# Three layers of a mixed transformer on one core: the last attention with stationary values and distant transposes, and the first squares added without waiting for the constants

## The reference

```python
def rms_norm(x, gain):
    xf = x.astype(jnp.float32)
    y = xf * lax.rsqrt(jnp.mean(xf * xf, axis=-1, keepdims=True) + RMS_EPS)
    return (y * gain.astype(jnp.float32)).astype(x.dtype)
...
    mod = jax.nn.silu(c) @ w_ada + b_ada
    shift, scale, gate = jnp.split(mod, 3, axis=-1)
    h = rms_norm_2(x, norm_g) * (1 + scale[:, None, :]) + shift[:, None, :]
    proj = h @ w_in
    q, kcr, vcr, ksl, vsl, kwn, vwn, z_a, g_br, u, z_s = jnp.split(proj, offs, axis=-1)
    gates = jax.nn.sigmoid(g_br).reshape(B, T, N_HEADS, N_BRANCH)
    attn = nsa_attention(q, kc, vc, k_slc, kv_heads(vsl), k_win, kv_heads(vwn), gates)
    # per head: g[0] * softmax(q kc) vc + g[1] * softmax(q_r k_slc) v_slc + g[2] * softmax(q_r k_win) v_win
    attn = attn * jax.nn.silu(z_a)
    y = gelu(s5_mixer(u, ...))
    y = y * jax.nn.sigmoid(y @ glu_w + glu_b)
    ssm = y * jax.nn.silu(z_s)
    mix = jnp.concatenate([attn, ssm], axis=-1) @ w_out
    return x + gate[:, None, :] * mix
```

## Time and profile before

| | |
|---|---|
| three runs, us | 1848.31, 1845.28, 1842.94; median 1845.28 |
| the profiled execution, us | 1844.67 |
| its span, us | 1842.5 |
| TensorE busy | 1760.9 us, 96% |
| VectorE busy | 1165.5 us, 63% |
| ScalarE busy | 667.8 us, 36% |
| GpSimd busy | 101.3 us, 5% |
| mean DMA | 134 GB/s |
| slab products (L474) in the chain that ended last | 70% |

### The profile page before, as it was taken

One profiled execution on the slowest core, in us unless ns is written; L12 is line 12 of the kernel. 1 busy time (PEld: TensorE's weight loads), 2 busy tenths in 40 slices (PEclk: granted clock), 3 DMA queues, 4 the chain that ended last, 5 costly groups with the idle time before them and its releaser, 6 DMA issues.

```text
span 1842.5 us, 24232 instructions
## 1 busy us (share of the span) xinstructions
PE 1760.9 (96%) x9361; PEld 1465.6 (80%) x9361; DVE 1165.5 (63%) x2373; ACT 667.8 (36%) x1081; POOL 101.3 (5%) x194
## 2 busy tenths in 40 slices
PE   3998999999999999999999999999999998999999
PEld 2776768888888888878888898888888987777787
DVE  6777766876467656564454548874676579445574
ACT  3423673423232333233232335322323332366432
POOL 0001100001000100100000000010001100000000
PEclk9999999999999999999999999999999999999999
DMA  9354324335333534642323224354336222300351
GB/s 367 115 181 162 115 69 145 138 114 186 120 115 136 172 114 155 212 164 92 137 91 138 75 97 146 135 171 164 140 129 201 96 91 92 127 34 24 138 195 46
DMA packets 45470, 245.98 MB, mean 134 GB/s; under 512 B 6256, under 2 KB 6480, under 8 KB 27440
## 3 DMA queue, kind: packets, MB, share of 16 engines
q1 hardware_dynamic: 24848, 155.36, 23.3%
q0 software_dynamic: 20512, 89.11, 14.4%
HBM read 229.23 MB, written 15.22 MB: 133 GB/s over the span
## 4 chain that ended last, share of the span: by engine, by line
PE 81%; DVE 11%; ACT 3%; issue 2%; DMA 2%; SPq 0%; DVEq 0%; ACTq 0%
PE ps L474 70%; DVE w_lo L1480 2%; PE ps L935 2%; DMA ada_raw<-in_ada 1%; PE ps L809 1%; PE ps L916 1%; PE ps L925 1%; ACT w_hi L1050 1%; PE ps L644 1%; DVE ada_raw L1504 1%; PE ps L667 1%; PE ps L653 1%; DVE ada_first L1865 1%; DVE pre L1597 1%; PE ps L957 1%
## 5 line engine op out<-in xcount | busy, mean ns | idle before, releaser
L1480 DVE TENSOR_TENSOR w_lo<-w_raw,w_hi 128x2048 fp32r<-128x2048 f32 x136 | 311.6, 2291 | 153.8 <-ACT w_hi L1050 153.5
L1050 ACT ACTIVATE w_hi<-w_raw 128x2048 fp32r<-128x2048 f32 x136 | 260.0, 1912 | 361.7 <-PE ps L474 339.0
L474 PE MATMUL ps<-h_hi,w_hi 128*128 128x512 f32 (+1 forms) x1008 | 379.1, 376 | 9.9 <-DVE w_lo L1480 6.5
L474 PE MATMUL ps<-h_lo,w_hi 128*128 128x512 f32 (+1 forms) x1008 | 374.8, 372 | 0.0
L474 PE MATMUL ps<-h_hi,w_lo 128*128 128x512 f32 (+1 forms) x1008 | 374.5, 372 | 0.0
L474 PEld LDWEIGHTS ps<-h_hi,w_hi 128*128 128x128 f32 x1008 | 191.8, 190 | 43.7 <-DVE w_lo L1480 7.0
L474 PEld LDWEIGHTS ps<-h_hi,w_lo 128*128 128x128 f32 x1008 | 191.7, 190 | 32.6
L474 PEld LDWEIGHTS ps<-h_lo,w_hi 128*128 128x128 f32 x1008 | 191.8, 190 | 31.3
L474 PE MATMUL ps<-hid_hi,w_hi 128*128 128x512 f32 (+1 forms) x576 | 211.3, 367 | 0.0
L474 PE MATMUL ps<-hid_hi,w_lo 128*128 128x512 f32 (+1 forms) x576 | 210.6, 366 | 0.0
L474 PE MATMUL ps<-hid_lo,w_hi 128*128 128x512 f32 (+1 forms) x576 | 210.5, 366 | 0.0
(11 more groups left out here) (395 smaller groups left out, 2400.5 us busy)
## 6 DMA issues: line engine op xcount, KB each, us to landing
w_raw<-in_slabs SPq DMA_DIRECT2D x136, 1024.0 KB, 4.8
ada_raw<-in_ada POOLq DMA_DIRECT2D x104, 512.0 KB, 5.1
s_tables<-s_tab POOLq DMA_DIRECT2D x4, 2692.0 KB, 9.2
s_t<-s_tables POOLq DMA_DIRECT2D x4, 2692.0 KB, 9.8
ada_first<-in_ada SPq DMA_DIRECT2D x16, 512.0 KB, 15.1
a_bias<-in_a_bias POOLq DMA_DIRECT2D x16, 256.0 KB, 3.3
xT<-in_xT SPq DMA_DIRECT2D x4, 512.0 KB, 6.3
s_toeplitz<-KTp POOLq DMA_DIRECT2D x32, 64.0 KB, 3.3
```

What stands on the lines that cost most here:

```text
L474: last = mm(o, l, r, start=start and n == 0, stop=stop and n == 2)
L1050: A(w_hi[s][:], w_raw[:, s, :], ACT.Copy).then_inc(sem("hi_done"), 1)
L1480: tt(w_lo[s][:], w_raw[:, s, :], w_hi[s][:].bitcast(F32), ALU.subtract).then_inc(sem("lo_done"), 1)
```

## The change

At the start VectorE adds squares as soon as they are there, and waits for the constants only before the first product with an ada tile; ScalarE's wait for `ones` and `eps` moves behind the squares and the silu.

In the last attention the weights are scaled by inverse sum and gate on VectorE before they are turned (as in the first loop), the values become the stationary side with 64 columns, and both groups of a head pair go to the two halves of a bank's partitions. All branches of a head pair add up in the same bank, the compressed one as the last (`compressed_out`, with scaled weights and a block-diagonal `vblk`). So the result stands turned in PSUM, `h_o`, its sums and its 16 transposes go, and gate, high and low part of three of the four head pairs move into the loop. The transposes stand six steps behind the scores instead of three, the values eight instead of four; there are 8 buffers for the exponentials. Slab units are cut into two bursts of 12. The steps of the turns of u and of the compressed branch are set anew. Output part 0 comes before the first block's outputs, and the rest is dealt out as 1, 2, 2, 1 and 1.

```diff
-        SIDE_A, SIDE_H = Side([0, 8, 14, 20, 26, 30, 34, 38], TT, 2), Side([1, 11, 22, 33, 44, 55], 2)
+        SIDE_A, SIDE_H = Side([0, 8, 14, 20, 26, 30, 34, 38], TT, 2), Side([1, 11, 22, 33, 44, 55], 2, 2)
...
+        U_STEPS = {step: (n // 3, n % 3) for n, step in enumerate((8, 16, 18, 20, 27, 29, 38, 40, 49, 51, 58, 60))}
+        CMP_STEPS = {step: (n // 2, n % 2) for n, step in enumerate((6, 14, 25, 31, 36, 42, 47, 53))}
+        CMP_SCALE = {step + 4: i for step, (i, part) in CMP_STEPS.items() if part == 0}
+        OUT_STEPS = {16 * i + 22: i for i in range(4)}
+        ATT_PARTS = (1,), (2, 3), (4, 5), (6,)
...
                 elif b == 1:
-                    gp.wait_ge(sem("h_added"), 4)
+                    gp.wait_ge(sem("c_out"), 4)
...
+            def compressed_out(i):
+
+                pe.wait_ge(sem("side_free"), C_COPIED[i])
+                for it in range(TT):
+                    last = mm(ps[5 + i % 2][:, it * P:(it + 1) * P], vblk[:, it % 2, :], c_pt[i % 2][:, it // 2, :],
+                              start=False, stop=True, skip_group_check=True)
+                last.then_inc(sem("c_out"), 1)
...
-                u = s - 3
+                u = s - 6
                 if 0 <= u < NUH:
...
-                u = s - 4
-                if 0 <= u < NUH:
-                    i, it, br, g = UNITS_H[u]
-                    pe.wait_ge(sem("hpt_ready"), u + 1)
-                    if u % 4 == 0 and u >= 8:
-                        pe.wait_ge(sem("ho_done"), u // 4 - 1)
-                    o, vc = ps[5 + u // 4 % 2][:, (u % 4) * HD:(u % 4 + 1) * HD], slice((br - 1) * P + g * HD, (br - 1) * P + (g + 1) * HD)
+                u = s - 8
+                if u >= 0 and s % 2 == 0:
+                    i, it, br, _ = UNITS_H[u]
+                    pe.wait_ge(sem("hpt_ready"), u + 2)
+                    if u % 16 == 0 and i >= 2:
+                        pe.wait_ge(sem("hxo_gated"), i - 1)
                     for j in range(it + 1):
-                        last = mm(o, h_pt[:, u % 3, j * P:(j + 1) * P], hv[:, j, vc], start=j == 0, stop=j == it)
+                        for g in range(H_GROUPS):
+                            vc = slice((br - 1) * P + g * HD, (br - 1) * P + (g + 1) * HD)
+                            last = mm(ps[5 + i % 2][HD * g:HD * g + HD, it * P:(it + 1) * P], hv[:, j, vc],
+                                      h_pt[:, (u + g) % 3, j * P:(j + 1) * P], start=it == 0 and br == 1 and j == 0, stop=False, skip_group_check=True)
                     last.then_inc(sem("ho_full"), 1)
+                if s in OUT_STEPS:
+                    compressed_out(OUT_STEPS[s])
...
             states(0)
-            pe.wait_ge(sem("h_added"), 4)
-            for i in range(4):
-                transposes([h_o[:, t, i * P:(i + 1) * P] for t in range(TT)], "hxo_full")
+            attention_part(0)
...
-            act.wait_ge(sem("ones_set"), 2)
             for k in range(KT):
...
             silu(0)
+            act.wait_ge(sem("ones_set"), 2)
+            A(stat[:, 8:9], eps[:], ACT.Sqrt)
             act.wait_ge(sem("consts_in"), 80)
-            A(stat[:, 8:9], eps[:], ACT.Sqrt)
...
-            dve.wait_ge(sem("consts_in"), 80)
-            dve.wait_ge(sem("ones_set"), 2)
             for k in range(1, KT):
...
             dve.wait_ge(sem("cond_done"), 1)
+            dve.wait_ge(sem("consts_in"), 80)
+            dve.wait_ge(sem("ones_set"), 2)
             first_pair(0)
...
+                u = s - 3
+                if 0 <= u < NUH and s % 2:
+                    i, it, br, _ = UNITS_H[u]
+                    n, h2 = P * (it + 1), slice(u % 8, u % 8 + 2)
+                    dve.wait_ge(sem("he_done"), u + 2)
+                    step(V.reciprocal(row_inv[:, h2], row_sum[:, h2]))
+                    step(tt(h_w[:, h2], row_inv[:, h2], h_gts[:, it, 6 * i:6 * i + 6].rearrange("p (g b) -> p g b", b=N_BR)[:, :, br], ALU.mult))
+                    for v in (u, u + 1):
+                        ts_(h_p[:, v % 8, 0:n], h_p[:, v % 8, 0:n], h_w[:, v % 8:v % 8 + 1], None, ALU.mult).then_inc(sem("hp_ready"), 1)
+                if s - 2 in OUT_STEPS:
+                    i = OUT_STEPS[s - 2]
+                    dve.wait_ge(sem("za_done"), 1)
+                    dve.wait_ge(sem("c_out"), i + 1)
+                    if i:
+                        dve.wait_ge(sem("hx_done"), i)
+                    tt(h_gate[:], ps[5 + i % 2][:], za[:, i, :], ALU.mult).then_inc(sem("hxo_gated"), 1)
+                if s - 4 in OUT_STEPS:
+                    i = OUT_STEPS[s - 4]
+                    dve.wait_ge(sem("hxo_hi"), i + 1)
+                    tt(o_lo[:, i, :], h_gate[:], o_hi[:, i, :].bitcast(F32), ALU.subtract).then_inc(sem("hx_done"), 1)
```

More of the change, by code:

```diff
@@ L349, in program @@
         ZA_READ = len(SIDE_A.starts) + 1 + H_USES.index(SIDE_H.starts[1]) + 1
+        C_COPIED = [len(SIDE_A.starts) + 1 + H_USES.index(step) + 1 for step, (i, part) in CMP_STEPS.items() if part == 1]
         SIDE_ALL = len(SIDE_A.starts) + 1 + len(H_USES)
@@ L902, in compressed @@
                     last.then_inc(sem("c_turned"), 1)
[L903 to L908, removed]
+            def compressed_out(i):
[4 more added lines that the diff above has]
+                last.then_inc(sem("c_out"), 1)
+            for s in range(NUH + 7):
                 if s < NUH and s % 2 == 0:
@@ L994, in _ @@
             states(0)
[L995 to L997 removed]
+            attention_part(0)
+            c.add("bank", 4)
             for blk in range(NBLK):
@@ L1387, in place_z @@
                 return za[:, 2 + u, :] if u < 2 else zs[:, u - 2, :]
-            for s in range(NUH + 3):
+            for s in range(NUH + 10):
                 side(SIDE_H, s, place_z)
@@ L2179, in _ @@
             kc = ps[7][0:CMP_PAD, :].rearrange("n (k g d) -> n k g d", k=4, d=HD)
-            step(cp(kcn[:], kc[:, 0, :, :]), *[cp(vblk[CMP_PAD * r:CMP_PAD * (r + 1), r, :], kc[:, 1, r % 2, :]) for r in range(4)])
+            step(cp(kcn[:], kc[:, 0, :, :]), *[cp(vblk[CMP_PAD * r:CMP_PAD * (r + 1), r // 2, HD * (r % 2):HD * (r % 2) + HD], kc[:, 1, r % 2, :]) for r in range(4)])
             V.engine_nop().then_inc(sem("side_free"), 1)
@@ L2184, in _ @@
             dve.wait_ge(sem("gts_done"), 1)
-            for s in range(NUH + 7):
+            for s in range(NUH + 11):
                 if s < NUH:
@@ L2207, in _ @@
                     V.engine_nop().then_inc(sem("side_free"), 1)
-                if s - 1 in CMP_STEPS:
-                    i, part = CMP_STEPS[s - 1]
+                if s - 1 in CMP_STEPS and CMP_STEPS[s - 1][1] == 0 or s in CMP_SCALE:
+                    i, part = (CMP_SCALE[s], 1) if s in CMP_SCALE else CMP_STEPS[s - 1]
                     cs = c_s[:].rearrange("p (j n) -> p j n", n=CMP_PAD)
@@ L2243, in _ @@
-                q = (s - 8) // 4
-                if s >= 8 and s % 4 == 0 and q < NUH // 4:
-                    i, it = UNITS_H[4 * q][0:2]
-                    dve.wait_ge(sem("hw_done"), q + 1)
-                    dve.wait_ge(sem("ho_full"), 4 * q + 4)
-                    step(tt(h_q4[:], ps[5 + q % 2][:, 0:256].rearrange("p (j d) -> p j d", d=HD),
-                            h_w[:, q % 2, :, :].rearrange("p b g -> p (b g)").unsqueeze(2).to_broadcast([P, 4, HD]), ALU.mult))
-                    tt(h_o[:, it, i * P:(i + 1) * P].rearrange("p (g d) -> p g d", d=HD), h_q4[:, 0:2, :], h_q4[:, 2:4, :], ALU.add)\
-                      .then_inc(sem("ho_done"), 1)
-                    dve.wait_ge(sem("ho_done"), q + 1)
@@ L2307, in _ @@
             recurrence(0)
-            dve.wait_ge(sem("za_done"), 1)
-            for i in range(5):
-                if i < 4:
-                    dve.wait_ge(sem("hxo_full"), i + 1)
-                    if i >= 2:
-                        dve.wait_ge(sem("hx_done"), i - 1)
-                    tt(h_gate[:, i % 2, :], ps_of(c)[:], za[:, i, :], ALU.mult).then_inc(sem("hxo_gated"), 1)
-                    c.add("bank")
-                if i:
-                    dve.wait_ge(sem("hxo_hi"), i)
-                    free(V.engine_nop())
-                    tt(o_lo[:, i - 1, :], h_gate[:, (i - 1) % 2, :], o_hi[:, i - 1, :].bitcast(F32), ALU.subtract).then_inc(sem("hx_done"), 1)
-            dve.wait_ge(sem("hx_done"), 4)
+            attention_part(0)
+            free(V.engine_nop(), 4)
+            c.add("bank", 4)
             for blk in range(NBLK):
```

109 lines of the change are left out of this document (39 added, 70 removed).

## The result

The changed kernel takes **1834.93 us** in the median of five runs (1833.21 to 1838.22), the kernel before 1845.28 (1842.94 to 1849.24): ratio 0.9937, 95% interval 0.9925 to 0.995. That is faster by about 10 us. The forecast was 1830.5, 1823 to 1838, so the time lies inside, 4.4 us above the point.

The account below looks back on a forecast made before the run. The prediction took TensorE, four fifths of the chain that ended last, as the bound. Start -4.1, last loop -8.5 and the stretch behind it -1.5 took 1844.67 to 1830.6, stated as 1830.5 us, range 1823 to 1838.

Parts of the forecast that it names:

- Start, -4.1: Start of the kernel: VectorE's adds no longer wait for the constants, and the shift reaches TensorE, -4.1 us.
- Rival 2: Start gives nothing, since a later transfer comes at its old time and VectorE waits for it: 1834.6 us, chance 0.06.
- Values, -13.4: Last attention loop: 320 value products of 128 columns in pairs replace 320 of 64 columns on TensorE, 35.8 to 22.4 us.
- Rival 4: Last loop: pairs overlap completely and changes between groups are free, 18.2 off instead of 7.9: 1820.3 us, chance 0.02.
- Transposes, +5.5: Last loop: 160 transposes in 64 groups get dearer on TensorE beside products in column halves, 21.4 to 26.9 us.
- Compressed and bursts, -1.4 and +0.6: Last loop: three compressed groups at 0.9 each stay, one leaves, -1.4 us; cutting six slab units adds six group changes, +0.6.
- Waits, +0.2: Last loop: TensorE's idle time, 6.1 us before, goes slightly up by 0.2, bounds -4 and +8.
- VectorE, 83 of 128: Last loop: VectorE has 83 us of work in some 128, covered by TensorE unless waited for step by step.
- Rival 3: Last loop: VectorE becomes the bound, waiting for ScalarE in each pair of steps; slower, for example 1852.3 us, chance 0.03.
- Rival 1: Middle of the last loop: VectorE's wait for exponentials sets the pace, waits of +8: 1838.4 us, chance 0.13.
- Rival 5: Last loop has the waits of the first attention loop or fewer, -3: 1827.6 us, chance 0.16.
- Behind the loop, -1.5: After the last loop: the second block's outputs start 23.15 us behind the last value instead of 24.7, -1.5 us.

Follow-up runs that it names:

- e1: The kernel before with only the start's edit (the moved waits for the constants and ones): 1842.44 us, ratio 0.9973.
- e12: The kernel of e2 run again, beside the changed kernel on the same chip: 1830.98 us, ratio to before 0.9914.
- e5: The changed kernel with the values' products of one group all before those of the other, not alternating between partition halves: 1841.9 us, ratio to before 0.9969.
- e7: The kernel of e2 with each slab unit as one burst of 24 products instead of two of 12: 1831.67 us, ratio to before 0.9925.
- e8: The kernel of e2 with each of VectorE's 64 weight scalings preceded by another of the same size by 1.0: 1839.3 us, ratio to before 0.9958.
- e2: The changed kernel with ScalarE's silu of z_a moved from step 14 to step 22 of the last loop: 1832.42 us, ratio to before 0.9917.
- e10: The kernel of e2 with transposes four steps behind the scores instead of six, values six instead of eight: 1835.33 us, ratio to before 0.9945.
- e3: The kernel before with the silu of z_a moved from step 13 to step 22 of the last loop: 1846.02 us, ratio 0.9986.
- e11: The changed kernel itself run again, nothing altered: 1835.8 us, ratio to before 0.9948.

## Why the prediction was right or wrong

**Start, -4.1, right.** Measured -3.6 at the first slab product and -3.9 at the loop, in most other profiles -4.0 to -4.1 at the product; e1 has it by itself. Rival 2, a transfer behind it, is out.

The terms of the loop can be measured one by one: TensorE's time from the first start of each group to that of the next, idle time taken out, added up by line from the first scores to the last value product. For the work I take e12, whose clock doesn't fall a second time; the last two rows are the changed kernel's own.

| term | forecast | before, us | after, us | change |
|---|---|---|---|---|
| values | -13.4 | 35.8 | 22.3 | -13.5 |
| transposes | +5.5 | 21.1 | 25.0 | +3.9 |
| compressed products | -1.4 | 4.05 | 2.9 | -1.2 |
| slab bursts | +0.6 | 35.3 | 36.4 | +1.0 |
| other work | 0 | 35.1 | 35.2 | +0.1 |
| waits | +0.2 | 7.0 | 9.9 | +2.9 |
| half clock at the silu | none | 0 | 2.6 | +2.6 |

**Values, -13.4, right.** 1.03 per sixteen. Rival 4, the pairs at 0.055 and changes between groups free, is out: a group of sixteen costs 1.03 and not 0.88. The Trainium skill, TensorEngine Tiling (Array Packing), section Theoretical Speedup, gives up to 2x for a side of 64 or less. The traces agree with the bound: in pairs a product takes 0.055 where one by itself takes 0.109 (e5), and a whole group of sixteen gains less, 1.03 for the 1.79 of before.

**Transposes, +5.5, too much by 1.6.** Four take 0.58 and no surplus appears in the pairs, but the 0.15 per group, read beside products in column halves, was taken for all 64 groups, and over the whole loop it is some 0.12.

**Compressed and bursts, -1.4 and +0.6, each off by 0.2 to 0.4** (1.00 for 0.9 a group; for the cut e7 has 0.3 in the loop).

**Waits, +0.2: this step failed.** It took the waits of before, 6.1, as a sum that moves little, and looked at the first loop for a sample. But 2.03 of them were one event, the silu of z_a with its table loads, which stands at a step and is covered by what TensorE has at that step. The change moved both: its text names the new steps of the turns of u and of the compressed branch, but not that of the silu, and neither text nor forecast asks what the silu would stand beside. The first loop has no such event, so it was no sample for it. Measured: waits of 4.06 instead of 2.03, and behind them 2.6 for the clock, 4.6 of added cost. The other waits rose by 0.9, where 0.2 was forecast; they moved from the readers of bank 7 (1.4, 0.5, 0.3 and 0.3 before) to VectorE's masks (2.9 after).

**The clock was not in the sum.** Each wait was priced at its length. At the silu 0.86 and 1.17 with 1.33 of work between them cost no more (before, and in e1 likewise); 1.89 and 2.17 with 0.52 of work between them cost 2.6 more.

**Some luck in the number.** Too dear transposes hid 0.9 of the miss, net of the other terms of work: waits and clock came 5.3 above the forecast, the loop 4.4.

**VectorE, 83 of 128, right:** 79.5. Rival 3 (VectorE sets the pace) is out by e8: 20.8 us more cost 4.5. Rival 1 (+8 in waits, in the middle) has the right sign and the wrong mechanism: one event and not the pace. Rival 5 (3 less in waits) didn't come: with the silu out of the way, in e12, TensorE is still idle for 5.0 in the window that had 6.1. That window is 126.2 for the 128.5 forecast because the silu's 2.0 are gone and the transposes are cheaper.

**Behind the loop, -1.5, right:** -1.4, with both outputs within 0.1 of the forecast.

So of the forecast's 14.1 us 9.4 came in the span of the profiled execution, and of the 4.7 missing ones 4.4 lie in the loop, most of them in one place of 14 us.

## What to carry to other kernels

Before a sum of waits is carried over, split it into events, and ask of each what covers it now and what will stand beside it afterwards; a long operation on another engine that is tied to a step (here a function with table loads) is such an event, and it belongs beside the longest burst of the bounding engine. A wait can have a second price, the clock behind it: here two waits of 1.89 and 2.17 joined by 0.52 of work cost 2.6 us more than their length. And a loop of the same shape is a good sample for prices of instructions, a rougher one for what a change between groups costs, and none for one-off work.

## What the runs showed of the hardware

The granted clock of TensorE falls to half (0.50, 1.2 GHz) behind stretches with waits, and the stretch differs between executions of the same code. At the start of the last loop it falls either with the first slab products (0.57 over 4 us in the changed kernel, 0.58 in e12) or some 10 us later, behind waits of 0.64, 0.40 and 0.72; the window of e2 there:

```profile
1605.70:1614.00 8.30, 6.66 (x28) 3.84 (x28) 6.99 (x34) 4.82 (x17) 0.00 (x0) 0.66 0.36 126
```

Where it falls with the slab products, the waits behind them are shorter (0.17, 0.15 and 0.76 in e12). The second form makes the loop 1.7 longer (129.2 in e2, 127.5 in e12, same kernel). The same happens elsewhere: from 1112 to 1120, between slabs, the changed kernel's first profile shows 1.00 and e12 0.62, and across that stretch e12 falls back by 1.5 us; its loop starts 3.7 later than the first profile's, though no instruction ahead of it differs. Behind the loop the same code with the same wait goes either way too: behind 1.87 the outputs take 5.38 in e2 and 7.05 in e8 and e10, behind 2.93 they take 5.38 in before and e1 and 7.05 in e3. This is a good part of the spread between executions (1833.95 to 1839.87 for the changed kernel in e11), and why a change of 2 us, as in e3, is read better from stretches of the trace than from medians. What decides between the two forms stays open: it wasn't tried.

Products into the two halves of the partitions overlap even when they are not issued in turn. In e5 the second head's first product starts 0.01 behind the first head's first in a group of four and four, and 0.01 behind its fifth in a group of eight and eight; in both it stands four behind that one in the order.
